# Three output tiles of a cross attention computed side by side, in pieces between its last heads

## The reference

```python
def memory_cross_attention(h, mem, wq, wkv, wo):
    q = (h @ wq).reshape(B, S, X_HEADS, X_HEAD_DIM)
    kv = mem @ wkv
    k = kv[..., :D_MODEL].reshape(B, M, X_HEADS, X_HEAD_DIM)
    v = kv[..., D_MODEL:].reshape(B, M, X_HEADS, X_HEAD_DIM)
    s = jnp.einsum('bshd,bmhd->bhsm', q, k).astype(jnp.float32) * (X_HEAD_DIM ** -0.5)
    p = jax.nn.softmax(s, axis=-1).astype(v.dtype)
    o = jnp.einsum('bhsm,bmhd->bshd', p, v).reshape(B, S, D_MODEL)
    return o @ wo
...
    h = h + memory_cross_attention(...)
    hn = rmsnorm(h, norm_ffn_g[l])
    gu = hn @ w_ffn_in[l]
```

## Time and profile before

| | us |
|---|---|
| median of 3 runs | 1338.28 |
| lowest and highest run | 1336.73, 1344.7 |
| the profiled execution | 1335.53 |
| its span in the profile | 1333.7 |
| TensorE busy | 1217.4 |
| VectorE busy | 807.6 |
| ScalarE busy | 583.0 |

### The profile page before, as it was taken

How to read it: one execution, slowest core, us unless ns; L and a number is a source line. 1 busy time by engine, 2 the same in 40 slices (tenths; PEclk the granted TensorE clock), 3 DMA queues, 4 the chain that set the end, 5 groups by cost and what they waited for, 6 DMA issues and landing times. The chain is left out here.

```text
span 1333.7 us, 22870 instructions
## 1 busy us (share of the span) xinstructions
PE 1217.4 (91%) x8638; PEld 1095.8 (82%) x8638; DVE 807.6 (61%) x1607; ACT 583.0 (44%) x1066; POOL 77.8 (6%) x87
## 2 busy tenths in 40 slices
PE   4999999989977898999999988999999879998986
PEld 4998899978977897988898977778776669887775
DVE  4865655558857755565665544655666557675764
ACT  4754444452221343533333434555555436554533
POOL 0410000003221000000000000000000000001000
PEclk9999999999988999999999988999999989889998
DMA  5554444433322452477885751121121115322110
GB/s 217 193 185 145 140 147 144 145 122 111 111 64 96 143 194 79 138 258 286 284 279 211 271 202 49 65 79 63 49 63 48 63 35 172 111 64 80 64 49 32
DMA packets 48398, 175.04 MB, mean 131 GB/s; under 512 B 5377, under 2 KB 6017, under 8 KB 47777
## 3 DMA queue, kind: packets, MB, share of 16 engines
q1 hardware_dynamic: 47664, 169.77, 37.8%
q0 software_dynamic: 624, 3.80, 0.8%
HBM read 172.50 MB, written 1.05 MB: 130 GB/s over the span
## 5 line engine op out<-in xcount | busy, mean ns | idle before, releaser
L1644 DVE TENSOR_TENSOR w_lo<-w_raw,w_hi 128x1024 fp32r<-128x1024 f32 (+1 forms) x272 | 331.0, 1223 | 227.0 <-ACT w_hi L1447 185.9
L1447 ACT CAST w_hi<-w_raw 128x1024 fp32r<-128x1024 f32 (+1 forms) x272 | 275.0, 1035 | 92.2 <-PE lin L1157 51.9
L1155 PE MATMUL lin<-XH,w_hi 128*128 128x256 f32 x448 | 130.0, 290 | 2.1 <-DVE w_lo L1644 2.1
L1156 PE MATMUL lin<-XL,w_hi 128*128 128x256 f32 x448 | 128.0, 286 | 0.0
L1157 PE MATMUL lin<-XH,w_lo 128*128 128x256 f32 x448 | 128.0, 286 | 0.0
L1155 PE MATMUL lin<-NH,w_hi 128*128 128x256 f32 x416 | 120.6, 290 | 1.3 <-DVE NL L1778 1.3
L1156 PE MATMUL lin<-NL,w_hi 128*128 128x256 f32 x416 | 117.8, 283 | 0.0
L1157 PE MATMUL lin<-NH,w_lo 128*128 128x256 f32 x416 | 117.7, 283 | 0.0
L1577 ACT ACTIVATE probs<-score,stat 128x512 f32<-128x512 f32 (+1 forms) x88 | 52.9, 606 | 116.7 <-DVE stat L1895 87.1
L1155 PEld LDWEIGHTS lin<-NH,w_hi 128*128 128x128 f32 x416 | 79.7, 192 | 14.4 <-issue 12.6
L1155 PEld LDWEIGHTS lin<-XH,w_hi 128*128 128x128 f32 x448 | 87.0, 194 | 5.0 <-issue 5.0
(11 more groups left out here) (370 smaller groups left out, 3175.2 us busy)
## 6 DMA issues: line engine op xcount, KB each, us to landing
w_raw<-in_ada SPq DMA_DIRECT2D x48, 512.0 KB, 5.4
w_raw<-in_w_out SPq DMA_DIRECT2D x32, 512.0 KB, 3.3
w_raw<-in_gate SPq DMA_DIRECT2D x22, 512.0 KB, 6.4
w_raw<-in_up SPq DMA_DIRECT2D x22, 512.0 KB, 3.7
w_raw<-in_ffn_out SPq DMA_DIRECT2D x16, 512.0 KB, 3.9
w_raw<-in_q SPq DMA_DIRECT2D x16, 512.0 KB, 3.4
w_raw<-in_z SPq DMA_DIRECT2D x16, 512.0 KB, 3.3
w_raw<-in_k SPq DMA_DIRECT2D x10, 512.0 KB, 3.3
```

Source lines behind the costliest of these rows:

```text
L1155: nc.tensor.matmul(bank[:, 0:W], wh, moving(H, kk), start=first, stop=False)
L1156: nc.tensor.matmul(bank[:, 0:W], wh, moving(L, kk), start=False, stop=False)
L1447: scal.copy(w_hi[:, i % HL, 0:n], raw[:, tile["i"] % RAW, 0:n]).then_inc(w_hi_ready, 1)
L1644: vec.tensor_sub(w_lo[:, i % HL, 0:n], raw[:, tile["i"] % RAW, 0:n], w_hi[:, i % HL, 0:n].bitcast(F32)).then_inc(w_lo_ready, 1)
```

## The change

`wo_x` tiles 0 to 2 are put side by side, with the loop over k outside, and this loop is cut into four pieces of two slices k, one for each head: the first at the `fill()` of head 2, the second at that of head 3, the third in a new `tail()` between the loop and the last `values`, the fourth where the stage stood before. Each piece waits for the heads whose slices it reads, no longer for all four. An `ahead` step stands before the first piece, so that the third tile's weights are split there. All three tiles must be split before the first piece. The evacuation of the three tiles, their squares and gains stay in `residual`, whose gain step now waits for its own tile instead of the newest.

```diff
-        def attention(new_units, fill, fill_first=False):
+        def attention(new_units, fill, fill_first=False, tail=None):
...
                 prev = cb
+            if tail:
+                tail()
             steps.append(("values", prev))
             steps.append(("values_out", prev))
...
-        def residual(stage, op, kts, gain, H, L, beside=None, ada_each=0):
+        def residual(stage, op, kts, gain, H, L, beside=None, ada_each=0, begun=()):
...
             for t in range(8):
                 ada_some(ada_each)
-                lin_step(stage, t, kts, True, op, T, ("add", hres))
+                if t < len(begun):
+                    steps.append(("lin", begun[t]))
+                else:
+                    lin_step(stage, t, kts, True, op, T, ("add", hres))
...
                 if gain:
-                    gain_step(t, hres[:, t, :], gain, H[:, t, :], L[:, t, :], ("g", n_lin[0] - 1))
+                    gain_step(t, hres[:, t, :], gain, H[:, t, :], L[:, t, :], ("g", lin_of[stage, t]))
...
+        heads_x, wo_three, wo_op = len(groups), [], operand(CH, CL)
+
+        def heads_part():
+
+            first = not wo_three
+            for t in range(3) if first else ():
+                lin_step("wo_x", t, DT, True, wo_op, T, ("add", hres))
+                wo_three.append(steps.pop()[1])
+                wo_three[-1].update(members=wo_three, heads=heads_x, k0=0)
+            if first:
+                steps.append(("ahead", {}))
+            k = wo_three[0]["k0"]
+            steps.append(("part", {"members": wo_three, "ks": range(k, k + 2)}))
+            wo_three[0]["k0"] = k + 2
+
         def fill_x():
             if q_todo:
                 q_x()
                 q_x()
-
-        attention([head_x(h) for h in range(X_HEADS)], fill_x)
-        N4, op4 = residual("wo_x", operand(CH, CL), DT, "norm_ffn", NH, NL)
+            else:
+                heads_part()
+
+        attention([head_x(h) for h in range(X_HEADS)], fill_x, tail=heads_part)
+        N4, op4 = residual("wo_x", wo_op, DT, "norm_ffn", NH, NL, begun=wo_three)
...
-                        side_by_side(s["members"])
+                        side_by_side(s["members"], range(s.get("k0", 0), DT))
...
+            def part(s):
+
+                side_by_side(s["members"], s["ks"])
+
-            def side_by_side(members):
+            def side_by_side(members, ks):
...
-                for k in range(DT):
+                for k in ks:
                     if op["ops"] is not None:
                         pe.wait_ge(op_ready, op["ops"][k])
+                    if "heads" in first:
+                        pe.wait_ge(heads_out, first["heads"] + k // 2 + 1)
```

More of the change, by code:

```diff
@@ L1360, in hvalues @@
                         last.then_inc(hg_pv, 1)
-            do = {"setup": setup, "lin": linear, "begin": begin, "sq": sq, "sqmm": sq, "bc": bc, "score_mm": score, "transp": transp,
+            do = {"setup": setup, "lin": linear, "begin": begin, "part": part, "sq": sq, "sqmm": sq, "bc": bc, "score_mm": score, "transp": transp,
                   "values": values, "hform": hform, "hvalues": hvalues, "adamm": adamm, "adaturn": adaturn}
```

## The result

| | before | after |
|---|---|---|
| median, us | 1338.28 | 1350.44 |
| lowest to highest | 1335.76 to 1344.7 (5 runs) | 1348.12 to 1353.66 (5 runs) |
| profiled execution | 1335.53 | 1350.44 |
| its span | 1333.7 | 1348.7 |

The ratio is 1.0086, with a 95% interval from 1.0064 to 1.0107: slower by about 12 us, twice what was forecast (+6.15) and outside the range by 1.4 us.

What follows compares the result with a forecast made beforehand. It took the first wo_x add plus a 24.46 us VectorE/ScalarE ring, not TensorE's queue, as the bound. That add 6.15 us later, with a full clock, gave 1338.28 + 6.15 = 1344.4 us; range 1338.5 to 1349.0.

Steps and rivals of the forecast that it cites:

- The sum in place: At the first residual add of wo_x: 538.94 us instead of 532.79, so 6.15 us later at full clock.
- the stall before the first piece: TensorE ahead of piece 1 waits for the third weight tile's low part: a new stall of 2.85 us.
- the last pause: TensorE's wait for the last head before the last piece stays whole: about 1.7 us, ended by `CL`.
- the pause behind the three tiles: TensorE after the three side by side tiles: about 3 us, ended by the fourth tile's `w_lo`.
- The likeliest case: In wo_x, the first add plus 24.46 us sets the feed forward start: +6.15 us, chance 0.50.
- TensorE's queue: Rival 3, in wo_x: TensorE's queue is the bound, only the fourth tile's start counts; +1.0 us, 1339.3, chance 0.07.
- the ring: In wo_x, VectorE and ScalarE's in-order chain of add, square, `NH`, cast, low part: 3.49 us a round against TensorE's 3.32.
- the likeliest sum: Whole kernel: +6.15 us at full clock, giving a median of 1344.4 us.
- rival 1: At piece 1 the clock falls in the first stall: 1.6 us more, +7.75 in all, 1346.0; chance 0.25.
- The row of `w_out0`: Evidence against a clock fall: behind its side by side tiles TensorE was busy 1.03 of 2 us at full clock.
- This stall is not added to the sum: Second stall, about 3 us before the fourth wo_x tile: costs nothing, its add not due before 549.4 us.
- `NL` and the feed forward part are 6.15 us late too: Behind wo_x: the eighth add comes at 563.40 us and the 6.15 us delay passes on, with nothing added.

Runs made afterwards that it cites:

- warm: Changed kernel plus 13 unread products on constants in TensorE's pause before the first piece; ratio to the kernel before 1.0062.
- after_ring: Changed kernel plus an ahead step behind each lin step of wo_x, and the fourth tile's weights split before the first add; ratio to the kernel before 1.0011.
- both: Changed kernel, third tile split in VectorE's pause, ahead step behind each wo_x lin step, fourth split before first add; ratios to the kernel before 0.9987, again 0.9991.
- uncut: Kernel before with wo_x tiles 0 to 2 side by side, uncut, all behind the last head; ratio to the kernel before 1.0097.
- ahead_only: Kernel before with only the third tile's weights split behind the exponentials of head 3, tiles one behind the other; ratio to the kernel before 1.0062.
- 9 copies: Kernel before with 9 chained scratch copies on VectorE ahead of the first add of wo_x, no product moved; ratio to the kernel before 1.0057.
- third_early: Changed kernel with the third wo_x tile's weights split between the last two q_x tiles, in a pause of VectorE; ratio to the kernel before 1.0054.
- 11 copies: Kernel before with 11 chained scratch copies on VectorE ahead of the first add of wo_x, no product moved; ratio to the kernel before 1.0090.
- 17 copies: Kernel before with 17 chained scratch copies on VectorE ahead of the first add of wo_x, no product moved; ratio to the kernel before 1.0088.

## Why the prediction was wrong

**The sum in place was right to 0.15 us, without the clock.** The first add was to be 6.15 us late. With the clock kept full (`warm`) it was 6.0 us late. Point by point: the stall before the first piece 2.85 forecast, 2.82 found; `values` of head 2 starts 1.38 us after its transpose, 1.32 forecast; the last pause 1.73, ended by `CL` as said; the pause behind the three tiles 2.96, "about 3" forecast. This last agreement is partly luck: the forecast had the pause end with the fourth tile's `w_lo`, but it ended with the square of the second tile, for whose column sums TensorE waits first. In the changed kernel `w_lo` was done at 543.86 + 1.22 = 545.08 us, and the sums started at 546.05. `after_ring` and `both` missed in part for this reason: an earlier `w_lo` leaves 1.23 us of the pause.

```profile
543.86 1.22 DVE L1672 TENSOR_TENSOR w_lo<-w_raw,w_hi 128x1024 fp32r<-128x1024 f32 x1 [0.51 <-ACT w_hi L1475]
```

The likeliest case, that the first add and not TensorE's queue sets the end, held in every kernel that left the ring as it was.

**The clock was left out of the likeliest sum** ("I leave it out of the likeliest sum and make it a rival"), with a chance of 0.25. It fell in both profiles of the changed kernel, and the first piece took 3.6 us instead of 2.2, 1.4 us more, where the forecast said 1.6. That is rival 1, and it was the case. The rule of the Trainium skill ("TensorE: Matmul & The Clock Gate", Part 1) that was weighed there, half clock as the state without activity, was on the right side: the traces agree, with 1.2 GHz behind the pauses of 2.82 us (changed kernel), 2.86 us (`uncut`) and 3.74 us (`ahead_only`). They also show that a pause of this kind need not be followed by it: with 9 copies TensorE stood 2.29 us, as long as in `br_hgrn`, and the clock stayed full.

```profile
540.52 0.61 PE L1258 MATMUL sum_bank<-ones,sqr 128*128 128x2 f32 x4 [2.29 <-ACT sqr L1487]
540.00:542.00 2.00, 1.48 (x12) 1.00 0.00 0
542.00:544.00 2.00, 2.00 (x18) 1.00 0.00 0
```

The row of `w_out0` in the earlier trace rows, by which I argued against it, has TensorE busy for 1.03 of 2 us, so it was not as empty as the pause before the first piece.

**"This stall is not added to the sum" was off by 0.4 us.** The fourth tile ran at half clock behind the second stall, its add waited 0.36 us for it, and the eighth add was 7.9 us late, not 7.5. The mechanism was as described; the slack of the fourth tile was taken at full clock.

**"`NL` and the feed forward part are 6.15 us late too", and with them everything behind, was the step that failed.** Up to 785 us it is right: the delay is passed on unchanged. Behind that the sum had no term, and 5.8 us came in the profile, 4.3 in the medians (12.2 - 7.9). Part of the difference between these two is that the profiled execution of before lies 2.75 us under its median. The forecast of 1344.4 was 6.0 us short: 1.4 for the first fall of the clock, 0.4 for the second, and the rest, about 4.2, for what came later; the windows of the profiles put that down to a lower granted clock (0.86, 0.98 and 0.95 in place of 0.91, 1.00 and 0.94). The total with 11 copies shows that a bare delay can bring such a loss without any product moved. What decides whether it comes stays open: it isn't monotonic in the delay (`after_ring`, with 4.2 us in place, costs 1.1 in all), and single executions differ in it without any difference in the kernel.

**The range and the chances.** The time moved by 0.86%, within 1% but only just, and the range ended 1.4 us below it. It took in the single causes one at a time. Rival 1 and a late effect together were not in it.

## What to carry to other kernels

Ask of each stage which chain of small steps goes from its first result to its end, and judge an edit by the moment of that first result. Tiles computed side by side share the wait for an operand but give their first result last; where the evacuation is a ring slower than the products (3.49 against 3.32 us here), that delay goes straight to the end, however busy TensorE is. Before an edit lets TensorE wait for work that an in-order list has placed late, work out a second price with the products behind the wait at half clock (here 1.4 us on 2.8, and 3.6 us on 2.45), and move the work that it waits for into a pause of the engine that does it (`third_early`: 5 us in place, for one step of the list).

## What the runs showed of the hardware

- A pause of TensorE of 2.82 us was followed by 3.2 us or so at half clock (0.21 us per 256 column product in place of 0.12), one of 3.74 us by some 10 us of it, with short pauses between. One of 2.27 us was followed by half clock, one of 2.29 us (9 copies) was not. Behind the same pauses of 0.29 and 1.23 us one execution of `both` fell to 0.63 and the other stayed at 1.00. Thirteen products on constants in the pause of 2.8 us kept the clock full.
- In the execution with 17 copies (8.2 us lost near 545 us), unchanged stages 250 to 560 us behind took 5.9 us longer, with a granted clock of 0.86, 0.98 and 0.95 in three windows, as in the changed kernel, against 0.91, 1.00 and 0.94 before. Over the fifteen other profiles of experiments and of the changed kernel this stretch takes from 2.3 us less to 10.0 us more than before, and neither the delay nor its absence foretells it.
- The kernel before, run again beside the experiments (93 runs), took from 1334.87 to 1346.1 us. Its mean granted clock went with the time: 0.969 in a run of 1335.18 us, 0.960 in one of 1346.1. The profiled execution, 1335.53 us, is near the fast end, so a comparison of two single profiles overstates the difference here by some 3 us.
